# A fourth buffer pair for split weight pieces in the eight experts of a two-block transformer kernel

## The reference, cut to what matters

```python
def swiglu(x, w1, w3, w2):
    return (jax.nn.silu(x @ w1) * (x @ w3)) @ w2

def moe_swiglu(x, router_w, w1, w3, w2):
    logits = (t @ router_w).astype(jnp.float32)
    top_v, top_i = lax.top_k(logits, TOP_K)          # 2 of 8
    gates = jax.nn.softmax(top_v, axis=-1)
    combine = jnp.sum(jax.nn.one_hot(top_i, N_EXPERTS, dtype=jnp.float32) * gates[..., None], axis=1)
    for e in range(N_EXPERTS):
        out = out + combine[:, e:e + 1] * swiglu(t, w1[e], w3[e], w2[e])
```

## Time and profile before

| | |
|---|---|
| median of 3 runs | 2150.57 us (2148.72 to 2155.72) |
| the profiled execution | 2145.45 us, span 2143.6 us |
| busy over the span | PE 93%, DVE 71%, ACT 51%, POOL 3% |
| DMA | 484 MB, 226 GB/s over the span |
| experts | from about 710 us to 1780 us of the span |
| an expert in form "a" (four of the five read) | 116.8 to 117.0 us |

### The profile page before, as it was taken

One profiled execution on the slowest core, in us unless ns is written; L12 is line 12 of the kernel. 1 busy time (PEld: TensorE's weight loads), 2 busy tenths in 40 slices (PEclk: granted clock), 3 DMA queues, 4 the chain that ended last, 5 costly groups with the idle time before them and its releaser, 6 DMA issues.

```text
span 2143.6 us, 25381 instructions
## 1 busy us (share of the span) xinstructions
PE 1996.8 (93%) x9950; PEld 1561.8 (73%) x9950; DVE 1512.1 (71%) x1834; ACT 1102.2 (51%) x1144; POOL 58.2 (3%) x64
## 2 busy tenths in 40 slices
PE   8889999999899899999999898888888898999997
PEld 7578588875695688878878766666666666659997
DVE  4665654457575555568888898989899897646666
ACT  1233243312240344447677687877777782544554
POOL 0120000000400000000000000000000000100000
PEclk9999999999999899999999999999999999999999
DMA  8202254532000766659989899999999994216450
GB/s 331 79 1 80 121 217 172 189 120 109 1 2 2 280 213 212 216 192 370 348 326 375 322 402 355 397 355 393 381 368 403 345 400 145 108 59 255 166 208 20
DMA packets 65019, 484.44 MB, mean 226 GB/s; under 512 B 9840, under 2 KB 12912, under 8 KB 13680
## 3 DMA queue, kind: packets, MB, share of 16 engines
q1 hardware_dynamic: 64880, 482.58, 59.7%
HBM read 481.51 MB, written 1.05 MB: 225 GB/s over the span
## 4 chain that ended last, share of the span: by engine, by line
PE 72%; DVE 13%; issue 7%; ACT 7%; DMA 1%; POOL 1%; SPq 0%; DVEq 0%; ACTq 0%; POOLq 0%
PE bank L622 12%; PE bank L993 11%; PE bank L995 11%; PE bank L994 11%; PE bank L998 7%; PE bank L999 6%; PE bank L825 5%; ACT e_hi L2360 4%; DVE e_lo L1898 4%; PE bank L1017 2%; PE bank L1077 2%; PE bank L629 1%; PE bank L786 1%; DVE b_arena L1413 1%; DVE e_h L1413 1%
## 5 line engine op out<-in xcount | busy, mean ns | idle before, releaser
L1898 DVE TENSOR_TENSOR e_lo<-b_ring,e_hi 128x2048 fp32r<-128x2048 f32 (+1 forms) x407 | 921.4, 2280 | 287.0 <-ACT e_hi L2360 286.1
L2360 ACT ACTIVATE e_hi<-b_ring 128x2048 fp32r<-128x2048 f32 (+1 forms) x407 | 772.1, 1909 | 201.3 <-PE bank L995 111.4
L998 PE MATMUL bank<-e_hi,e_x 128*128 128x512 f32 x672 | 279.8, 416 | 33.0 <-DVE e_lo L1898 23.1
L999 PE MATMUL bank<-e_lo,e_x 128*128 128x512 f32 x672 | 266.1, 396 | 0.0
L993 PE MATMUL bank<-e_hi,e_x 128*128 128x512 f32 (+1 forms) x528 | 208.4, 395 | 4.5 <-DVE e_lo L1898 2.6
L994 PE MATMUL bank<-e_lo,e_x 128*128 128x512 f32 (+1 forms) x528 | 202.9, 384 | 0.0
L995 PE MATMUL bank<-e_hi,e_x 128*128 128x512 f32 (+1 forms) x528 | 202.8, 384 | 0.0
L998 PEld LDWEIGHTS bank<-e_hi,e_x 128*128 128x128 f32 x672 | 127.9, 190 | 100.7 <-DVE e_lo L1898 59.6
L998 PE MATMUL bank<-e_hi,e_th 128*128 128x512 f32 x336 | 137.9, 411 | 20.4 <-DVE e_lo L1898 20.0
L999 PEld LDWEIGHTS bank<-e_lo,e_x 128*128 128x128 f32 x672 | 128.1, 191 | 25.4 <-issue 1.6
L993 PE MATMUL bank<-e_hi,e_th 128*128 128x512 f32 x352 | 137.7, 391 | 0.4 <-DVE e_tl L1902 0.4
(11 more groups left out here) (268 smaller groups left out, 2853.3 us busy)
## 6 DMA issues: line engine op xcount, KB each, us to landing
b_ring<-in_moe_w SPq DMA_DIRECT2D x336, 1024.0 KB, 6.9
b_ring<-in_ffn_w SPq DMA_DIRECT2D x15, 2048.0 KB, 8.3
b_ring<-in_w_in SPq DMA_DIRECT2D x14, 2048.0 KB, 8.4
b_ring<-in_w_up SPq DMA_DIRECT2D x12, 2048.0 KB, 8.3
b_ring<-in_w_down SPq DMA_DIRECT2D x6, 2048.0 KB, 8.6
b_ring<-in_w_o SPq DMA_DIRECT2D x4, 2048.0 KB, 8.3
b_gain<-in_gains SPq DMA_DIRECT2D x6, 1024.0 KB, 4.6
b_ring<-in_w_out SPq DMA_DIRECT2D x2, 2048.0 KB, 8.2
```

The lines of the kernel that those rows point to most:

```text
L998: e.matmul(out, both, bh, start=first, stop=False)
L999: return e.matmul(out, both, bl, start=False, stop=last)
L1898: e.tensor_tensor(lo, raw, r32(hi), ALU.subtract).then_inc(lo_dve.sem)
L2360: return e.activation(out, x, ACT.Copy)
```

## The change

One more pair of buffers, `spare_hi` and `spare_lo`, exists while the experts run. It lies in the memory of `gain` and of the part of the constants that the mixers alone use, which is now a tensor `masks` with a DMA of its own. With the spare pair the pieces of the experts rotate over four pairs (`place`, `last_in_place`), and the split at the step of piece p is that of piece p+3 (`lead`). The dense feed-forward part of layer 0 and that of the second block keep three pairs and a lead of two. The load of the last `gain` of the first block moves from ahead of the experts to the end of the last expert, behind a wait for its piece 38, and the load of `n1` gets its own semaphore. Ahead of expert 0, ACT and DVE split three pieces in place of two.

```diff
+        with ExitStack() as over:
+            gain, masks = (over.enter_context(nc.sbuf_tensor("b_" + n, [128, 2048], F32)) for n in ("gain", "masks"))
+        spare = [sb("spare_hi", [128, 2048], F32R), sb("spare_lo", [128, 2048], F32R)]
...
+            moe_hi, moe_lo = ([spare[j], *(b[j] for b in split)] for j in range(2))
...
+        def last_in_place(p):
+
+            if MOE_P <= p < FF2_P:
+                return max(p - NH - 1, MOE_P - 1)
+            return max(p - NH, FF2_P - 1) if p >= FF2_P else p - NH
+
+        def lead(at):
+            return NH if MOE_P <= at < FF2_P else NH - 1
+
         def place(p):
 
-            return (p + (p >= MOE_P)) % NH
+            return (p - MOE_P) % (NH + 1) if MOE_P <= p < FF2_P else p % NH
...
-                        if p + 2 < ends:
-                            split_rest(p + 2)
+                        if p + lead(at) < ends:
+                            split_rest(p + lead(at))
...
-                split_rest(MOE_P)
-                split_rest(MOE_P + 1)
+                for i in range(NH):
+                    split_rest(MOE_P + i)
...
-                if p >= NH:
-                    e.wait_ge(*piece(p - NH))
+                if last_in_place(p) >= 0:
+                    e.wait_ge(*piece(last_in_place(p)))
...
-                        if p + 2 < ends:
-                            split_round(p + 2)
+                        if p + lead(at) < ends:
+                            split_round(p + lead(at))
...
-                split_round(MOE_P)
-                split_round(MOE_P + 1)
+                e.wait_ge(*ln_out(2))
+                for i in range(NH):
+                    split_round(MOE_P + i)
...
-            e.dma_start(cst[:, 128:CTOT], a["cst"][:, 128:CTOT]).then_inc(s_c, 16)
+            e.dma_start(cst[:, 128:CMASK], a["cst"][:, 128:CMASK]).then_inc(s_c, 16)
+            e.dma_start(masks[:, :], a["cst"][:, CMASK:CTOT]).then_inc(s_c, 16)
...
-            load_gain(3, ln_out(2))
...
+            load(IN2_AT + 2)
+            load_gain(3, piece(FF2_P - 4))
             load(IN2_AT + 4)
```

More of the change, by code:

```diff
@@ L25 @@
 LEVELS = 7
-CONSTS = ["ident", "ones", "mean256", "tri0", "tri1", "before", "bt0", "bt1", "iota", "pairs", "most"] + \
-    [f"m{d}{k}" for d in range(2) for k in range(LEVELS)] + ["c1", "s1", "c2", "s2"]
+CONSTS = ["ident", "ones", "mean256", "tri0", "tri1", "before", "iota", "pairs", "most", "c1", "s1", "c2", "s2"] + \
+    ["bt0", "bt1"] + [f"m{d}{k}" for d in range(2) for k in range(LEVELS)]
 CWIDTH = {"iota": 256, "most": 8, "c1": 128, "s1": 128, "c2": 128, "s2": 128}
@@ L34 @@
     _at += CWIDTH.get(_n, 128)
-CTOT = _at
+CTOT, CMASK = _at, CAT["bt0"]
+assert CTOT - CMASK == 2048
 def layout(parts):
@@ L319, in C @@
         def C(name):
-            return cst[:, CAT[name]:CAT[name] + CWIDTH.get(name, 128)]
+            of, o = (masks, CAT[name] - CMASK) if CAT[name] >= CMASK else (cst, CAT[name])
+            return of[:, o:o + CWIDTH.get(name, 128)]
         def col(name, i):
@@ L396, in two_blocks @@
         s_half = [sem(f"half{i}") for i in range(NR)]
-        s_x, s_x1, s_first, s_id, s_c, s_cols, s_rows, s_gain, s_ba, s_pw, s_rw, s_bd, s_out = (
-            sem(n) for n in ("x", "x1", "first", "id", "c", "cols", "rows", "gain", "ba", "pw", "rw", "bd", "out"))
+        s_x, s_x1, s_first, s_id, s_c, s_cols, s_rows, s_gain, s_n1, s_ba, s_pw, s_rw, s_bd, s_out = (
+            sem(n) for n in ("x", "x1", "first", "id", "c", "cols", "rows", "gain", "n1", "ba", "pw", "rw", "bd", "out"))
         def ring_in(n):
@@ L584, in two_blocks, with hi_of, lo_of @@
             pieces.append((ring_in(n), raw, 2048))
-        def place(p):
-            return (p + (p >= MOE_P)) % NH
+        def last_in_place(p):
[4 more added lines that the diff above has]
+            return NH if MOE_P <= at < FF2_P else NH - 1
+        def place(p):
+            return (p - MOE_P) % (NH + 1) if MOE_P <= p < FF2_P else p % NH
+        def hi_of(p):
+            return (moe_hi if MOE_P <= p < FF2_P else e_hi)[place(p)]
+        def lo_of(p):
+            return (moe_lo if MOE_P <= p < FF2_P else e_lo)[place(p)]
         def split_views(p):
             _, raw, size = pieces[p]
-            hi, lo = e_hi[place(p)][:, 0:size], e_lo[place(p)][:, 0:size]
+            hi, lo = hi_of(p)[:, 0:size], lo_of(p)[:, 0:size]
             if len(raw.shape) == 3:
@@ L983, in mixer @@
                 mixer_front(l)
-                e.wait_ge(s_c, 16)
+                e.wait_ge(s_c, 32)
                 e.wait_ge(*kq_out(l))
@@ L1002, in take_piece @@
                 e.wait_ge(*lo_dve(p))
-                return e_hi[place(p)], e_lo[place(p)]
+                return hi_of(p), lo_of(p)
             def gated(widths, at, unit, kinds, first=None, aside=None, where=(0, 1)):
@@ L1501, in rms_gain @@
             def rms_gain(rnd, outs, g, ts_):
-                e.wait_ge(s_gain, 16 * (5 + rnd))
+                e.wait_ge(*((s_n1, 16) if rnd == 0 else (s_gain, 16 * (4 + rnd))))
                 for t in ts_:
@@ L2113, in aside @@
                         picks(ex + 1, 0, 2)
-                gated(FFE_UNITS, at, 6 + 7 * ex, kinds, at + 42 + 2 * more, aside)
+                gated(FFE_UNITS, at, 6 + 7 * ex, kinds, at + 42 + lead(at) * more, aside)
                 e.wait_ge(*piece(at + 41))
```

11 lines of the change are left out of this document (5 added, 6 removed).

## The result

| | before | changed |
|---|---|---|
| median | 2152.07 us (2148.72 to 2155.72, 4 runs) | 2189.53 us (2188.64 to 2195.45, 4 runs) |
| ratio | | 1.0188, 95% interval 1.0169 to 1.0207 |
| profiled span | 2143.6 us | 2187.1 us |

The change makes the kernel 1.9% slower. The forecast was 2113 us, 1.8% faster, in a range of 2098 to 2135 us.

What follows compares the result with a forecast made beforehand. It took a ring of PE, ACT and DVE to bound experts 3 to 7. From a median of 2150.57 us, -36.8 (unit stalls), -3.3 (expert changes) and +2.6 (start of expert 0) gave 2113 us, range 2098 to 2135.

Steps and rivals of the forecast that it cites:

- What bounds the kernel: Experts 3 to 7, 575 us: neither PE nor DVE full, DVE idle 50.4 us, almost all of it waiting for ACT's rounding.
- a ring of three engines: Experts 3 to 7: PE frees a buffer, ACT rounds into it, DVE takes the rest, PE multiplies; a unit takes 15.47 us.
- The extra piece in hand: Units of experts 3 to 7: one more rounded piece ahead removes both DVE stalls of each unit, -36.8 us.
- no effect: Rival for the units: ACT's list order, not buffers, sets the stalls, so they remain; 2153 us, chance 0.10.
- slower: Rival for the units: transfers lose rate when asked for more, below 407 GB/s units lengthen; 2201 us at 374, chance 0.05.
- At the changes of expert: Around the five changes of expert: one in four of the 0.9 to 1.1 us stalls goes, -3.3 us.
- The start of expert 0: Ahead of expert 0: a third piece to split delays PE's gather for the second tile, +2.6 us.
- Nothing for experts 0 to 2, the constants and `gain`: Experts 0 to 2 gain nothing, and moving the constants and the `gain` load costs nothing.
- Whether DMA can follow: Weight loads in experts 3 to 7: the ring's reserve covers the need, 405 GB/s over an expert, so no loss.
- The size of the gain: Whole kernel: the terms -36.8, -3.3 and +2.6 sum to -37.5 us, with DVE's unit at 14.42 us.

Runs made afterwards that it cites:

- e4_two_ahead: Changed kernel with its four buffer pairs and memory moves, but both splits two pieces ahead as before; 2145.84 us, ratio 0.9994 to the kernel before.
- e1_rest_first: Changed kernel with DVE taking the rest at T ahead of the preceding step's split; 2129.68 us, ratio 0.9918 to the kernel before.
- e2_dummies: Changed kernel with two unread matmuls ahead of PE's wait for T's rest, in form "a"; 2164.99 us, ratio 1.0077 to the kernel before.
- e5_both_first: Changed kernel with DVE taking both the rest at T and the product of gate and value ahead of a split; 2099.76 us, ratio 0.9779.
- e3_round_ahead: Changed kernel with ACT rounding three pieces ahead but DVE taking rests only two ahead; 2099.18 us, ratio 0.9777 to the kernel before.
- e6: Changed kernel with DVE making the product of gate and value ahead of the step's split; 2140.77 us, ratio 0.9967 to the kernel before.
- e7: Changed kernel with ACT three pieces ahead, DVE two, and only three rest buffers; 2092.46 us, ratio 0.9747 to the kernel before.
- e8: Kernel before, no buffer added, with DVE making the product ahead of the step's split in all experts; 2134.11 us, ratio 0.9928.
- e9: Kernel before, no buffer added, with DVE making the product ahead of the step's split in form "a" alone; 2123.00 us, ratio 0.9878.

## Why the prediction was wrong

**What bounds the kernel** was read rightly: experts 3 to 7, no full engine, a ring of three engines. The description of that ring was not. "PE frees a buffer, ACT rounds into it" is no part of the loop: e4_two_ahead has the free buffer and the same unit. ACT's 0.82 us wait for a buffer is real but beside the path. I had read waits, which name the last thing an engine waited for, and not the chain of waits over one period, which had the loop in it.

**"The extra piece in hand"** is the step that failed, forecast -36.8 us. Its durations were about right; what was wrong is the sentence that each stall has a margin because DVE has 2.20 us more work ahead of it. The work in hand was won by putting one more split ahead of two results that PE waits for. The diff and the order of instructions showed this, and the section on the change said so of both the product and the rest; the prediction looked at the product only. It dismissed the rival "no effect" by "the turn needs the product of gate and value, which DVE makes no later than PE reaches T", though the earlier trace rows list ten waits of PE's turn for that product, 13.6 us, and it never asked who waits for the rest at T. PE does, ahead of w3, for the bank. That stand cost nothing before because the rest came in time. Undoing it alone gives 58 us against the changed kernel (e1_rest_first). What the runs show in its place: 0 us a unit from the loop, and +31.9 us from TensorE's clock.

**The clock** was no term of the sum at all. Rows of before gave 0.99 to 1.00 over the experts, and nothing in the forecast asked what a regular pause of PE would do to it. The rival "slower" had the right sign with the wrong mechanism: it asked for transfers under 407 GB/s that make units longer. In the unit of 15.50 us shown above the rate is 425. The unit of 17.00 us has 402, but e2_dummies, which only gives PE two more matmuls in a unit, brings such units back to 15.39 us at 420, so there the rate follows the unit.

**At the changes of expert**, forecast -3.3: no gain there. PE's wait for the product rose from 13.6 us in 575 to 18.9 in 605, ten times each. In e5_both_first and e3_round_ahead, where the product is in its place, experts 4 to 6 shrink by 9.4 to 11.1 us. Seven units at 15.45 - 14.14 = 1.31 us are 9.2 us of it, which leaves 0.2 to 1.9 us an expert for the changes. The 0.7 us forecast lies in that, but it was a guess of one stall in four, so that is luck.

**The start of expert 0**, forecast +2.6, measured +3.6. The timeline of ACT and DVE there in the changed kernel, which answers the earlier trace rows:

```profile
726.65 1.91 ACT L2380 ACTIVATE e_hi<-b_ring 128x2048 fp32r<-128x2048 f32 x1 [2.02 <-DMA b_ring<-in_moe_w]
```
```profile
728.59 2.29 DVE L1918 TENSOR_TENSOR e_lo<-b_ring,e_hi 128x2048 fp32r<-128x2048 f32 x1 [1.63 <-ACT e_hi L2380]
730.80 0.49 DVE L1439 SCALAR_TENSOR_TENSOR e_P<-e_folded,b_rank 128x128 f32<-128x128 f32 x2
```

The third rounding does wait for its landing, and the third rest stands ahead of `e_P`. From the router's matmuls to the second gather it is 28.8 to 29.3 us in the five kernels with three rests there (changed, e1, e2, e5, e6), 26.6 to 27.0 in the three with two rests and four buffers for rounded pieces (e3, e4, e7), and 25.0 to 25.3 in those with the program of before (before, e8, e9). The 1.4 us or so by which the middle group is longer than the last don't lie at the splits, but ahead of the first gather, where the clock was halved for 13.7 us on end in these three executions and for 6.8 in the other eight. From the first gather of expert 0 to the second it is 11.8 to 12.2 us in e3, e4 and e7, 12.0 to 12.2 with the program of before, and 15.8 to 16.3 with three rests. So the third split cost all of the 3.6 us. The mechanism was right, and the term that was too small is the spacing of the landings: the third rounding started 3.9 us behind the second, not 2.5, and DVE stood 1.6 us for it.

**Nothing for experts 0 to 2, the constants and `gain`**: right (-0.2 us, and e4_two_ahead's ratio of 0.9994).

**Whether DMA can follow**: right. With DVE never waiting for it, an expert ran at 413 GB/s, above the 405 that the prediction asked for, and among ACT's waits from 1203 to 1730 us there is none for a landing (e3_round_ahead). The figure of about 358 GB/s for a core in the Trainium skill, "DMA: Bandwidth & Descriptors", section Specifications, would have put an expert at 44.04 MB / 358 = 123 us, an estimate. The changed kernel's expert 5 took just that, 123.0 us at 359 GB/s, and a reader could take this for the limit reached. It is a coincidence: e3_round_ahead moves the same bytes in 107 us. The same page's section Bandwidth has 425 GB/s for a core alone. The trace agrees: 425 GB/s in the unit of 15.50 us above.

**The size of the gain** where the idea works: forecast -37.5 us, measured -47.2 (e3_round_ahead, 2146.37 to 2099.18). DVE's own unit is 14.14 us and not 14.42, since a split that follows another directly adds 2.20 us and one behind a stop 2.29. That is 35 x 0.28 = 9.8 us, about the whole difference.

Open: the first 5.7 us, ahead of the experts. The profiled executions reach the router's matmuls between 694.6 and 702.6 us, with stretches of halved clock at different places. e8_before_product_first has the program of before up to there and arrives at 702.6, the kernel before at 696.9, so I don't put this to the change.

## What to carry to other kernels

A buffer more does nothing by itself where no wait for a free buffer is in the loop (ratio 0.9994). It can still be what lets an engine's work move ahead in its list (0.9747), and then the order is what has to be worked out: follow the chain of waits over one period, name every link, and see which links are dependences and which are only places in an engine's list. When a lead grows, every small result that shares the list with the long operations moves back by one of them; list these results, ask who waits for each, a bank that is about to be overwritten included, and put them ahead. Let only that engine run ahead whose lateness is in the loop, here ACT's rounding, and limit an order to the stage whose bound it fits: the product first gained 4 us in each expert bound by DVE and lost 3.5 in those bound by PE.

## What the runs showed of the hardware

In the changed kernel TensorE's granted clock fell to half for 3.4 us behind 20 of the 25 pauses for the rest at T, sixteen of 2.5 us and four of 1.8, which came once a unit. In e6_product_first it did so behind 13 of 30 pauses of 1.1 to 2.0 us, none of them shorter than 1.8. Not every pause did it: behind the first for T's rest of each expert of the changed kernel, 2.5 us long, it stayed whole. Such a stretch cost a unit 1.57 us, since PE's first piece of w3 and `pairs`, which ran in it, are on the loop. With the pause filled by two matmuls, so that 0.6 us were left of it, the clock stayed whole in every steady unit. By the lengths of the units, the lost clock is the whole of the changed kernel's loss in experts 3 to 7.
